# A deeper ring for the second gathered tile's U rows, later expert choices for the third, and three first-tile products an item

## The reference, cut to what matters

```
scores = q . sub_keys                       # 8 heads, 2 x 128 keys each
top 16 of 128 in each half, top 16 of the 16x16 sums   -> ids, gates
act = gelu(sum_d x1[t, d] * u_tab[ids[t, k], d]) * gate[t, k]     # 128 experts a token
out = layer_norm(alpha * x1 + sum_k act[t, k] * v_tab[ids[t, k], :])
```

## Time and profile before

| what | us |
|---|---|
| median of 3 runs (3256.12 to 3261.7) | 3259.27 |
| the profiled execution, its time | 3262.99 |
| its span in the trace | 3261.2 |
| TensorE busy | 2669.5 (82%) |
| VectorE busy | 2201.8 (68%) |
| GpSimd busy | 1482.6 (45%) |

### The profile page before, as it was taken

How to read it: one execution, slowest core, us unless ns; L and a number is a source line. 1 busy time by engine, 2 the same in 40 slices (tenths; PEclk the granted TensorE clock), 3 DMA queues, 4 the chain that set the end, 5 groups by cost and what they waited for, 6 DMA issues and landing times.

```text
span 3261.2 us, 30907 instructions
## 1 busy us (share of the span) xinstructions
PE 2669.5 (82%) x9137; PEld 1364.6 (42%) x9137; DVE 2201.8 (68%) x4895; ACT 559.1 (17%) x1267; POOL 1482.6 (45%) x1333
## 2 busy tenths in 40 slices
PE   8999994675668887657689999999999987878883
PEld 3454542443324555423334444444444443434441
DVE  3334577867648788678845766744444688888888
ACT  1231101332103777400000000100000000000000
POOL 0011004445334222344565555566656576675773
PEclk9999996887888899878889999999999989889996
DMA  4213226555479898898999999899999999999995
GB/s 146 87 52 139 91 84 231 178 199 194 187 285 344 310 331 320 296 358 313 331 394 373 385 376 404 326 407 398 396 404 397 377 407 407 406 407 371 404 409 191
DMA packets 310549, 987.81 MB, mean 303 GB/s; under 512 B 29936, under 2 KB 57840, under 8 KB 309616
## 3 DMA queue, kind: packets, MB, share of 16 engines
q0 software_dynamic: 184320, 671.17, 54.1%
q1 hardware_dynamic: 123440, 314.21, 25.6%
q10 hardware_dynamic: 2624, 0.46, 0.1%
HBM read 947.98 MB, written 37.75 MB: 302 GB/s over the span
## 4 chain that ended last, share of the span: by engine, by line
PE 24%; issue 15%; POOL 14%; DMA 10%; DVE 5%; ACT 2%; DVEq 1%; ACTq 1%; PEld 0%; POOLq 0%; PEldq 0%
POOL u_ring L1994 9%; PE part L2090 7%; PE hid L2071 6%; PE turn_ps L2063 4%; DMA v_ring<-in_peer_v_dram,ids_t 4%; PE acc L2128 4%; POOL v_ring L2021 4%; DMA v_ring<-in_peer_v_dram,ids_u 2%; DVE x_rows_in L2317 2%; POOL v_ring L2007 2%; PE part L2099 1%; ACT dense_sums L2168 1%; DMA u_ring<-in_peer_u_dram,ids_u 1%; DMA u_ring<-in_peer_v_dram,ids_t 1%; ACT dense_sums L2170 1%
## 5 line engine op out<-in xcount | busy, mean ns | idle before, releaser
L2090 PE MATMUL part<-room 128*128 128x512 f32 x1536 | 716.4, 618 | 198.1 <-DVE room L2398 186.2
L2422 DVE CUSTOM_DVE_ANT_0 u_ring<-u_ring,x_rows_in 128x1024 f32<-128x1024 f32 x512 | 618.7, 1223 | 314.9 <-DMA u_ring<-in_peer_u_dram,ids_u 305.2
L1994 POOL DMA_INDIRECT u_ring<-in_peer_u_dram,ids_u x512 | 580.0, 1133 | 469.3 <-DVE dots L2422 327.1
L2071 PE MATMUL hid<-x1t_dense,room 128*128 128x384 f32 x2048 | 692.6, 492 | 5.8 <-DMA room<-in_peer_ut_dram 4.6
L2007 POOL DMA_INDIRECT v_ring<-in_peer_v_dram,ids_t x344 | 368.1, 1070 | 384.3 <-PE acc L2128 269.9
L2090 PEld LDWEIGHTS part<-room 128*128 128x128 f32 x1536 | 302.2, 199 | 565.6 <-issue 346.0
L2071 PEld LDWEIGHTS hid<-x1t_dense,room 128*128 128x128 f32 x2048 | 387.4, 192 | 320.9 <-issue 80.8
L2317 DVE SCALAR_TENSOR_TENSOR x_rows_in<-v_ring,coef,x_rows_in 128x1024 f32<-128x1024 f32 x208 | 267.1, 1284 | 63.8 <-DMA v_ring<-in_peer_v_dram,ids_u 50.1
L2206 ACT ACTIVATE room<-hid 128x384 f32<-128x384 f32 x128 | 62.7, 490 | 1435.0 <-PE hid L2071 1435.0
L2021 POOL DMA_INDIRECT v_ring<-in_peer_v_dram,ids_u x208 | 234.7, 1129 | 76.5 <-issue 58.5
L1165 POOL DMA_INDIRECT u_rows<-in_peer_u_dram,ids_first x123 | 153.0, 1244 | 186.7 <-POOLq L1164 160.9
(11 more groups left out here) (368 smaller groups left out, 2809.0 us busy)
## 6 DMA issues: line engine op xcount, KB each, us to landing
room<-in_peer_ut_dram SPq DMA_DIRECT2D x128, 512.0 KB, 7.0
room<-in_peer_v_dram SPq DMA_DIRECT2D x128, 512.0 KB, 9.7
wq_pair<-in_peer_wq_dram SPq DMA_DIRECT2D x25, 2048.0 KB, 19.0
gate_grid<-room SPq DMA_DIRECT2D x6, 4096.0 KB, 13.8
room<-gate_grid SPq DMA_DIRECT2D x32, 768.0 KB, 17.3
w_ring<-in_w_in_dram SPq DMA_DIRECT2D x10, 2048.0 KB, 7.9
w_ring<-in_w_out_dram SPq DMA_DIRECT2D x4, 2048.0 KB, 8.2
u_ring<-in_peer_u_dram,ids_u POOLq DMA_INDIRECT x512, 10.6
```

The costliest lines, as they stand in the source:

```text
L1994: pool.indirect_dma_start(u_ring[:, n % U_RING, :], None, peer_u, bass.IndirectOffsetOnAxis(ap=ids_u[:, q, k:k + 1], axis=0))\
L2071: last = mm.matmul(hid[:, 0:DT], ud[:, c % UD_RING, k, :], x1td[:, k, :], start=(k == 0), stop=(k == KC - 1))
L2090: last = mm.matmul(part[k % 3][:], weights[:, n % 2, i, d * P:(d + 1) * P], vd[:, slot, half * 512:(half + 1) * 512], start=(i == 0), stop ...
L2422: vec.tensor_tensor_reduce(u_ring[:, n % U_RING, :], u_ring[:, n % U_RING, :], x1[:, q % 2, :], 1.0, 0.0, ALU.mult, ALU.add, dots[:, q % 2 ...
```

## The change

Three edits in the code.

1. In the mixer `products(n)` holds three rows for each of the 28 items and four a step after that, so the 128 products lie in n = 0 to 38; `SPARE_FROM` becomes 3 * 28 + 8 = 92.
2. U rows 0 to 127 of the experts' part (those of q = 1) use a ring of 13 places, the five U places and the eight V places; later rows use five again. A row waits for the product of the row that was in its place before. The waits on landed rows are counted anew, and the first V quads of q = 1 (`WIDE_QUADS`, `WIDE_QUADS` + 1) wait until all 128 of these products are done.
3. Tile 5 is chosen in steps 28, 32, 36, 40, tile 6 in 43 to 61 and tile 7 in 46 to 64. VectorE signals each pair (`pairs_chosen`), and GpSimd waits before every 32nd row for that pair instead of for the whole tile.

```diff
-        SPARE_FROM = 4 * (items + 2)
+        SPARE_FROM = 3 * items + 4 * 2
+        def products_by(n):
+            return 3 * min(n, items) + 4 * max(n - items, 0)
         def products(n):
-            return range(min(4 * n, FIRST_SLOTS), min(4 * n + 4, FIRST_SLOTS))
+            return range(min(products_by(n), FIRST_SLOTS), min(products_by(n + 1), FIRST_SLOTS))
...
-CHOSEN_AT = {1: 0, 2: 4, 3: 8, 4: 12, 5: 20, 6: 40, 7: 43}
-PAIR_STEPS = {1: 1, 2: 1, 3: 1, 4: 1, 5: 3, 6: 6, 7: 6}
+CHOSEN_AT = {1: 0, 2: 4, 3: 8, 4: 12, 5: 28, 6: 43, 7: 46}
+PAIR_STEPS = {1: 1, 2: 1, 3: 1, 4: 1, 5: 4, 6: 6, 7: 6}
...
+DEEP_ROWS = SLOTS
+DEEP_RING = U_RING + V_RING
+def u_place(n):
+    return n % DEEP_RING if n < DEEP_ROWS else n % U_RING
+def u_rows_in(place, rows):
+    return sum(u_place(n) == place for n in range(rows))
 def u_uses(n):
-    slot = n % U_RING
-    return n // U_RING + 1 + (wide_uses(2) if n >= U_BASE[1] and slot < 4 else 0)
+    place = u_place(n)
+    quads = wide_uses(2) * (place < 4) if place < U_RING else wide_uses((place - U_RING) // 4)
+    return u_rows_in(place, n + 1) + quads
+def row_before(n):
+    return max((m for m in range(n) if u_place(m) == u_place(n)), default=None)
+def turn_of(t, pair):
+    return next(n for n, turn in enumerate(TURNS) if turn[1:] == (t, pair))
...
             def gather_u(n, q, k):
-                if n >= U_RING:
-                    pool.wait_ge(u_used, n - U_RING + 1)
+                if row_before(n) is not None:
+                    pool.wait_ge(u_used, row_before(n) + 1)
...
             def gather_v(m, q, s, j):
...
+                if m in (WIDE_QUADS, WIDE_QUADS + 1):
+                    pool.wait_ge(u_used, DEEP_ROWS)
...
-                        if k == 0:
-                            pool.wait_ge(tiles_chosen, list(CHOSEN_AT).index(GATHERED[q]) + 1)
+                        if k % (2 * TOPK) == 0:
+                            pool.wait_ge(pairs_chosen, turn_of(GATHERED[q], k // (2 * TOPK)) + 1)
...
-                        if turn[0] == 3 and turn[3] == PAIRS - 1:
-                            dve.sem_inc(tiles_chosen, 1)
+                        if turn[0] == 3:
+                            dve.sem_inc(pairs_chosen, 1)
```

More of the change, by code:

```diff
@@ L1552, in summed_slot @@
         tiles_before = sum(SLOTS // V_RING for _ in range(FIRST_SUMMED, q))
-        return i, wide_uses(i // 4) + (QUADS * FIRST_SUMMED - WIDE_QUADS) // 2 + tiles_before + use
+        return i, wide_uses(i // 4) + u_rows_in(U_RING + i, DEEP_ROWS) + (QUADS * FIRST_SUMMED - WIDE_QUADS) // 2 + tiles_before + use
     j = i - V_RING
-    return i, u_rows_landed(LAST_WIDE, j) + (wide_uses(2) if j < 4 else 0) + use
+    return i, u_rows_in(j, U_BASE[-1] + SLOTS) + (wide_uses(2) if j < 4 else 0) + use
 def v_slots(m):
@@ L1564, in v_slots @@
     return group, wide_uses(group) + use + 1, m - 1 if use else last + 1
-def u_rows_landed(m, j):
-    rows = U_BASE[1] if m < WIDE_QUADS else U_BASE[-1] + SLOTS
-    return (rows - j + U_RING - 1) // U_RING
-def u_uses(n):
-    slot = n % U_RING
-    return n // U_RING + 1 + (wide_uses(2) if n >= U_BASE[1] and slot < 4 else 0)
+DEEP_ROWS = SLOTS
[4 more added lines that the diff above has]
+    return sum(u_place(n) == place for n in range(rows))
+def u_uses(n):
+    place = u_place(n)
[3 more added lines that the diff above has]
+    return max((m for m in range(n) if u_place(m) == u_place(n)), default=None)
 def share(items, i, n):
@@ L1814, in build_experts @@
         stage_stored = [sem(f"stage_stored{i}_e") for i in range(2)]
-        tiles_chosen = sem("tiles_chosen_e")
+        pairs_chosen = sem("pairs_chosen_e")
         ids_t_ready = sem("ids_t_ready_e")
@@ L1836, in build_experts, with u_row, u_row_landed @@
         consts = sem("consts2_e")
+        def u_row(n):
+            place = u_place(n)
+            return u_ring[:, place, :] if place < U_RING else v_ring[:, place - U_RING, :]
+        def u_row_landed(n):
+            place = u_place(n)
+            return u_landed[place] if place < U_RING else v_landed[place - U_RING]
         def last_row(i):
@@ L1989, in gather_u @@
             def gather_u(n, q, k):
-                if n >= U_RING:
-                    pool.wait_ge(u_used, n - U_RING + 1)
+                if row_before(n) is not None:
+                    pool.wait_ge(u_used, row_before(n) + 1)
                 if n >= U_BASE[1]:
                     pool.wait_ge(quads_used, WIDE_QUADS)
-                pool.indirect_dma_start(u_ring[:, n % U_RING, :], None, peer_u,
+                pool.indirect_dma_start(u_row(n), None, peer_u,
                                         bass.IndirectOffsetOnAxis(ap=ids_u[:, q, k:k + 1], axis=0))\
-                    .then_inc(u_landed[n % U_RING], 16)
+                    .then_inc(u_row_landed(n), 16)
             def gather_v(m, q, s, j):
@@ L2120, in _ @@
                             if group < 2:
-                                pe.wait_ge(v_landed[4 * group + j], uses * 16)
+                                deep = u_rows_in(U_RING + 4 * group + j, DEEP_ROWS) if m >= WIDE_QUADS else 0
+                                pe.wait_ge(v_landed[4 * group + j], (deep + uses) * 16)
                             else:
-                                pe.wait_ge(u_landed[j], (u_rows_landed(m, j) + uses) * 16)
+                                pe.wait_ge(u_landed[j], uses * 16)
                         for half in range(2):
@@ L2420, in _ @@
                             dve.wait_ge(x1_in[q % 2], (q // 2 + 1) * 16)
-                        dve.wait_ge(u_landed[n % U_RING], u_uses(n) * 16)
-                        vec.tensor_tensor_reduce(u_ring[:, n % U_RING, :], u_ring[:, n % U_RING, :], x1[:, q % 2, :], 1.0, 0.0,
+                        dve.wait_ge(u_row_landed(n), u_uses(n) * 16)
+                        vec.tensor_tensor_reduce(u_row(n), u_row(n), x1[:, q % 2, :], 1.0, 0.0,
                                                  ALU.mult, ALU.add, dots[:, q % 2, k:k + 1]).then_inc(u_used, 1)
```

## The result

The changed kernel takes **3235.16 us** (median of 4 runs, 3230.96 to 3238.82), the kernel before 3259.00 (4 runs, 3256.12 to 3261.7) beside it: ratio 0.9922 [0.9907, 0.9936], 24 us faster where 43 was forecast. The profiled execution of after took 3230.96, 32.0 less than that of before. Of these 32.0, 5.3 lie ahead of everything that the change touches (the mixer's item part begins at 507.22 us instead of 512.52), which leaves 26.7 to explain.

The account below looks back on a forecast made before the run. Transfers bound it from step 67, TensorE in steps 43 to 66, a latency loop through five places in 18 to 33. Terms -7 - 4 - 58 + 10 + 16 = -43 from 3263.0 gave 3220, median 3216; range 3192 to 3247 us.

Parts of the forecast that it names:

- Products in the mixer: Mixer: taking products out of items saves 19 us, the tail costs 12; net -7 us, between -19 and +12.
- First gathers of q = 1: Before step 18: gathers no longer wait for tile 4's last pair, shortening the first products' wait; -4 us, between -5 and 0.
- Thirteen places and two choices fewer: Steps 18 to 33: more places and less choice work cut 288 us to 230; -58 us, between -75 and -45.
- By bytes: Steps 18 to 33: limit from transferred data, 85.6 MB at 402 GB/s, 213 us.
- bound by pace: Steps 18 to 33: transfer limit from 13.2 us a step, plus loads; 243 us.
- Hand-over: Step 34: V rows wait for the last product and stand ahead of U rows; +10 us, between 0 and 33.
- Two more choices after step 34: After step 34: choices add work to TensorE and transfers, VectorE has room; +16 us, between +6 and +18.
- After step 67: From step 67 on: transfers set the pace and their bytes stay, so nothing changes; 0 us.
- The signs: Steps 18 to 34 and mixer: some 230 us at 395 GB/s, two waits below 30 us, first gather near 1300 us.
- The slower rival: Steps 18 to 33: busy VectorE stretches gathers to 2.17 us, GpSimd sets the pace; +5 us or +24, chance 0.08.
- The ring does not do what it says: Steps 18 to 33: transfers already full, rows only land later; +3 us in all, 3262, chance 0.06.
- the transfers give more: Steps 18 to 33 take 213 us and the step 34 hand-over costs 0; -74 us, 3185, chance 0.10.

Follow-up runs that it names:

- the mixer alone: Changed kernel with only its new spread of mixer products, five places and the old choice steps kept: 3255.65 us, 0.9980 of the kernel before.
- The early gathers: Changed kernel, tile 5 chosen every three steps, tiles 6, 7 from 40, 43; first thirteen U rows await only their own places' quads: 3217.55 us, ratio 0.9863.
- The two singles: Two kernels, the ring alone and the choices alone, each with one part of the change: ratios 0.9916 and 1.0006 to the kernel before.
- the ring alone: Changed kernel with only the thirteen places, old mixer products and old choice steps kept: 3234.06 us, 0.9916 of the kernel before.
- The choices alone: Changed kernel with only the later choices, signalled pair by pair; five places and old mixer kept: 3261.61 us, 1.0006 of the kernel before.

## Why the prediction was right, and where it was off

The direction, the main mechanism and its size were right; the gain was put at 43 us and is 24. By the steps of the prediction:

- **Products in the mixer, -7: the net was near.** The profiles give -3.9 in after and -7.0 in the mixer alone. From the first maxima to the last (833.18 before, 812.16 after) it is -15.7 where I had -19, and from there to the next block's start 91.8 instead of 80.0 us, +11.8 where I had +12.
- **First gathers of q = 1, -4: this step failed.** I held the wait for the last pair of tile 4 to be what ended the idleness, and named the last quad among the new conditions without asking when it comes. In before the two ended together: the last quad at 1323.62 us, the pair's indices at 1323.75. The change lifted the one and left the other: the first gather stands after 31.32 us of idleness (31.36 before), and the way from the mixer's end to step 18 fell by 1.5 us. The early gathers, which lift the quad's wait too, show what I had in mind: 5.4 us on that way.
- **Thirteen places and two choices fewer, -58: -54.1.** 230 us expected and 234.4 found, 395 GB/s and 393. The two singles, 35.0 and 21.2, add up to 56.2. That 230 was so near is in part luck, as I picked it between bounds of which two were off. By bytes I had 85.6 MB with fifteen gathers fewer; only eight fewer came (111 instead of 119), and 393 GB/s over 234.4 us are 92.1 MB. The base of my bound by pace was wrong, too: the mark at 2576.60 is that of step 99, not 100, so that stage is 13.6 us a step instead of 13.2, and the bound 249 instead of 243.
- **Hand-over, +10: this step failed.** VectorE did reach the coefficients late, 16.4 us after step 34's mark (1595.09 us) instead of 10.5; in the ring alone it is 13.2 (1618.83), and steps 34 to 67 of that kernel cost 1 us more than before. So 2.7 us of lateness, not 10, belong to the ring's own order of gathers, and the lower bound of 0 was nearly the answer. The other 3 us appear only together with the moved choices: there the last product of q = 1 ends nearer to the mark, and the first V gather, which waits for it, stands 0.5 us behind the mark instead of 1.9 ahead of it. For TensorE little changes, since it waited for these coefficients already: 15.8 us in before, 17.3 in after, 13.6 in the ring alone. In after, the first V gather stands behind the last product and VectorE behind a U row:

```profile
1579.16 0.93 POOL L2040 DMA_INDIRECT v_ring<-in_peer_v_dram,ids_t  x1 [21.36 <-DVE dots L2456]
```
```profile
1588.29 1.23 DVE L2456 CUSTOM_DVE_ANT_0 u_ring<-u_ring,x_rows_in 128x1024 f32<-128x1024 f32 x1 [8.57 <-DMA u_ring<-in_peer_u_dram,ids_u]
...
1595.09 0.28 DVE L2338 TENSOR_TENSOR coef<-dots,gates 128x128 f32<-128x128 f32 x1
```

- **Two more choices after step 34, +16: too small.** The choices alone, without any new hand-over, cost 24.4 us from 34 to 67 and 5.7 in step 67. I priced them by TensorE's extra work, 17.8 us, and that came at 20.4. I gave VectorE's part no cost, since it was 44 busy of 103 us there. That average hid one place, steps 64 to 67, where the shifted last choice of tile 7 meets a normalisation and the coefficients, and TensorE waits 8.4 us for these. TensorE idles 9.6 us more from 34 to 68 by the choices alone, 6.5 of them in steps 60 to 67.
- **Hand-over and choices together** were forecast at +26 for steps 34 to 67 and came at +27.8: two errors that cancel, which a look at the total alone would have counted as a hit.
- **After step 67, 0: +5.0,** of it 5.8 in step 67 itself.

The sum in the profiles, start of the item part aside, is -26.7 against -43. The 16.3 us between them are 3.1 of the mixer, 2.5 of the first gathers, 3.9 of steps 18 to 33, 1.8 of steps 34 to 66 and 5.0 of what follows: no term failed by much in sum, and all of them fell on the same side. The medians differ by 23.8, the profiles by 32.0: executions of one kernel differ by a few us, and the profiled one of after was the fastest of its four.

**The signs** that the prediction named were met in part. VectorE's wait for U rows is 36.0 us and TensorE's for the weighting 35.6, both forecast below 30; the first gather did not move to 1300 us. The forecast's bounds, put at 3195 and 3240, are 3189 and 3252 when both ends are taken together.

**The slower rival** (GpSimd at 2.17 us a gather) did not come: 111 gathers in steps 18 to 33 have medians of 0.979 and 1.012 us, and maxima of 1.99. The long form is there, 1.87 + 0.30 us at 1319.12, but beside products and not, as the prediction has it, beside token marks. The 34 gathers of over 1.5 us in these steps all began while a product ran, and each ended 0.81 us after it (1318.96 + 1.22 + 0.81 = 1319.12 + 1.87); the 31 that began while VectorE ran nothing took 0.93 to 0.94 us. The rule of the Trainium skill, "SBUF — State Buffer", section "SBUF: two separate sides", agrees with these gathers: it has one of the two engines wait for the other's whole instruction, among others where VectorE's has two inputs in SBUF and GpSimd's reads SBUF. A VectorE busy for 178 of 234 us did not make that the pace: a gather took 141.23/111 = 1.27 us on average, and half of them under 1.02. **"The ring does not do what it says"** is refuted by the ring alone, **"the transfers give more"** by steps 18 to 33 at 234 us: the DMA share is 1.01 and there is nothing left to give at this amount of bytes.

## What to carry to other kernels

A producer that waits for places, a consumer that waits for rows and a pipe that is not full are one loop: places divided by latency bounds its rate. Here eight more places gave 35.0 us, and 36 us of work taken off the consumer gave 21.2. Stop adding when the DMA share reaches 1; from there, rows here mostly landed later (16.5 us instead of 11.5, for 3.7 us of time). When work moves to a stage that looks idle on average, list what the engine does at the very steps where it lands: at the end of a tile's work, with a normalisation and the coefficients that another engine waits for, room on average was worth nothing, and the choice cost 6.3 us of idleness on top of its 10.2 us of work. Where two waits end within 0.3 us of each other, the profile names one of them; lifting that one alone gained nothing here.

## What was not expected of the hardware

- **Landing time follows the depth.** Gathers of the same size landed a median 8.2 us after issue with five places at 341 GB/s, 11.5 with nine at 394, 16.5 with thirteen at 393, and 19.0 in the ring alone (thirteen, four choices beside it) at 383. A latency read from a short ring is no constant to plan a long one with.
- **The same code starts at different times.** The mixer's item part began between 506.69 and 512.55 us in 13 profiled executions, with nothing changed ahead of it. Stages, not absolute marks, are what two profiles can be compared by.
